# Early output tiles, the opening's loads in another order, and the opening joined with the first projection in one block

## The reference

```python
def first_block(x, c, ...):
    c_act = silu(c)
    for l in range(2):
        mod = c_act @ w_ada[l] + b_ada[l]
        shift, scale, gate = split(mod, 3)
        h = rms_norm(x, norm_g[l]) * (1.0 + scale) + shift
        proj = h @ w_in[l]
        gq, gk, gv, glr, gz, dq, dk, dv, dz = split_columns(proj)
        gq, gk, gv = split(silu(causal_depthwise_conv(concat(gq, gk, gv), conv_w[l])))
        o_gla = gla_branch(gq, gk, gv, glr, gz, ...)       # chunked gated linear attention
        lam = exp(sum(lam_q1 * lam_k1)) - exp(sum(lam_q2 * lam_k2)) + lam_init
        o_diff = diff_branch(dq, dk, dv, dz, ..., lam)     # softmax(map 0) - lam * softmax(map 1)
        x = x + gate * (concat(o_gla, o_diff) @ w_out[l])
    return x

def second_block(x, ...):        # MLA attention, short convolution and SSD side by side, then a gated FFN
    ...
```

## Time and profile before

| | before |
|---|---|
| median of 3 runs | 2401.17 us |
| profiled execution, its own time | 2397.69 us |
| its span | 2395.6 us |
| mean granted clock of PE | 0.997 |
| PE busy | 2314.5 us (97%) |
| DVE busy | 1263.4 us (53%) |
| ScalarE busy | 1064.2 us (44%) |
| GpSimd busy | 596.3 us (25%) |

### The profile page before, as it was taken

How to read it: one execution, slowest core, us unless ns; L and a number is a source line. 1 busy time by engine, 2 the same in 40 slices (tenths; PEclk the granted TensorE clock), 3 DMA queues, 4 the chain that set the end, 5 groups by cost and what they waited for, 6 DMA issues and landing times. The chain is left out here.

```text
span 2395.6 us, 33130 instructions
## 1 busy us (share of the span) xinstructions
PE 2314.5 (97%) x12824; PEld 1888.7 (79%) x12824; DVE 1263.4 (53%) x1776; ACT 1064.2 (44%) x2262; POOL 596.3 (25%) x411
## 2 busy tenths in 40 slices
PE   6999999989999999999999999999999999999999
PEld 4787787778887777777888887677888888888887
DVE  5855304874644411785551366660787777774121
ACT  4445333774534433575443445553653333334221
POOL 2200020232400021132332121212214444465130
PEclk9999999999999999999999999999999999999999
DMA  7442110104112111103211100003222222236231
GB/s 254 132 133 80 36 53 1 36 2 166 62 44 98 45 53 36 35 2 124 88 53 30 58 1 5 23 10 132 89 81 95 80 79 80 94 134 245 89 132 44
DMA packets 139073, 181.87 MB, mean 76 GB/s; under 512 B 8700, under 2 KB 102307, under 8 KB 138917
## 3 DMA queue, kind: packets, MB, share of 16 engines
q1 hardware_dynamic: 137877, 179.74, 22.2%
q10 hardware_dynamic: 1040, 0.00, 0.0%
HBM read 151.41 MB, written 28.31 MB: 75 GB/s over the span
## 5 line engine op out<-in xcount | busy, mean ns | idle before, releaser
L825 PE MATMUL ps<-w_hi,hT_hi 128*128 128x512 f32 (+1 forms) x384 | 142.2, 370 | 2.1 <-PEq L683 1.0
L825 PE MATMUL ps<-hT_hi,w_hi 128*128 128x512 f32 x360 | 141.2, 392 | 2.8 <-PEq L275 2.8
L825 PE MATMUL ps<-w_lo,hT_hi 128*128 128x512 f32 (+1 forms) x384 | 142.1, 370 | 0.0
L825 PE MATMUL ps<-w_hi,hT_lo 128*128 128x512 f32 (+1 forms) x384 | 142.0, 370 | 0.0
L825 PE MATMUL ps<-hT_lo,w_hi 128*128 128x512 f32 x360 | 140.6, 390 | 0.0
L4093 POOL TENSOR_TENSOR w_lo<-ffn_sums,w_hi 128x512 fp32r<-128x512 f32 x76 | 96.7, 1293 | 172.1 <-ACT w_hi L4275 172.1
L756 POOL TENSOR_TENSOR w_lo<-difp_raw,w_hi 128x2048 fp32r<-128x2048 f32 x8 | 36.8, 4603 | 386.6 <-ACT w_hi L725 386.6
L825 PE MATMUL ps<-hT_hi,w_lo 128*128 128x512 f32 x328 | 128.4, 391 | 0.0
L4143 PE MATMUL ps<-ffn_t_hi,w_hi 128*128 128x512 f32 x304 | 118.4, 389 | 0.7 <-DVE ffn_u L4452 0.7
L4143 PE MATMUL ps<-ffn_t_hi,w_lo 128*128 128x512 f32 x304 | 118.3, 389 | 0.0
L4143 PE MATMUL ps<-ffn_t_lo,w_hi 128*128 128x512 f32 x304 | 118.3, 389 | 0.0
(11 more groups left out here) (575 smaller groups left out, 6477.3 us busy)
## 6 DMA issues: line engine op xcount, KB each, us to landing
ffn_raw<-in_ffn_w_up SPq DMA_DIRECT2D x40, 512.0 KB, 4.8
mix_gla<-in_w_ada SPq DMA_DIRECT2D x32, 512.0 KB, 3.5
ffn_raw<-in_ffn_w_down SPq DMA_DIRECT2D x30, 512.0 KB, 4.6
xres<-big SPq DMA_DIRECT2D x24, 512.0 KB, 2.6
hid<-ffn_f SPq DMA_DIRECT2D x22, 512.0 KB, 2.6
ffn_sums<-hid SPq DMA_DIRECT2D x44, 256.0 KB, 3.9
glap_raw<-in_w_in SPq DMA_DIRECT2D x10, 1024.0 KB, 5.2
difp_raw<-in_w_in SPq DMA_DIRECT2D x10, 1024.0 KB, 5.0
```

The source lines that it names most:

```text
L825: mm = nc.tensor.matmul(out, l, r, start=(job.part != 1 and c == 0 and k == 0), stop=(job.evac and c == job.chunks - 1 and k == len(pairs) ...
```

## The change

Three things are changed.

*The attention's end.* `OUT_EARLY` becomes the list (4, 5, 0): PE does the GLA half of output tiles 4, 5 and 0 inside the attention stage. Tile 4 is cut into four pieces of three matmuls (one feature chunk each): one ahead of the turns of rounds 21, 22 and 23 of PE's loop, one behind the loop. Tile 5 stands behind `turn_y(6)`, tile 0 is cut in two halves around `turn_y(7)`. The tiles are split in the order (4, 0, 5, 1, 2, 3, 6, 7); ScalarE converts the first two (4 and 0) in rounds 15 and 16 of its loop, where GpSimd, not DVE, subtracts them.

*The opening's loads.* SP issues `w_ada` 4 and 5 before the lambda rows, then the second weight tile, `w_ada` 6 and 7, and the small rows of the second block last. ScalarE's `weight(1)` stands between the partial sums 4 and 5.

*One block.* The opening and the projection of layer 0 share a block. The new `OpenSeam` carries the waits of the projection: PE's first two units wait for feature chunks 6 and 7 of the first token half alone (14 of the 16 units), from unit 2 on for all 16, from unit 4 on for the second weight tile, the turned small rows and the gains; the other engines wait for everything. Job 0 of layer 0 goes by token halves (spread).

```diff
@@ -29,7 +29,7 @@
 RIGHT = "right"
-OUT_EARLY = 2
+OUT_EARLY = (4, 5, 0)
 PLAIN_EARLY = (4, 5, 0)
@@ -263,7 +263,38 @@
-def stage_open(nc, m, a, x, layer_rows, lam_rows, lam_src, jobs):
+class OpenSeam:
+
+
+    def __init__(self, s_hi, s_lov, s_lop, s_wlo, s_gain, s_later, groups):
+        self.s_hi, self.s_lov, self.s_lop, self.s_wlo, self.s_gain = s_hi, s_lov, s_lop, s_wlo, s_gain
+        self.s_later, self.groups = s_later, groups
+
+    def split(self, eng, units):
+        eng.wait_ge(self.s_hi, units)
+        eng.wait_ge(self.s_lov, units // 2)
+        eng.wait_ge(self.s_lop, units // 2)
+
+    def settled(self, eng):
+        self.split(eng, 2 * KC)
+        eng.wait_ge(self.s_wlo, 8)
+        eng.wait_ge(self.s_later, self.groups)
+
+    def staging_free(self, sp):
+        self.settled(sp)
+
+    def before(self, pe, g, half):
+        if g == 0:
+            self.split(pe, 2 * KC - 2)
+        if g == 2:
+            self.split(pe, 2 * KC)
+        if g == 4:
+            pe.wait_ge(self.s_wlo, 8)
+            pe.wait_ge(self.s_later, self.groups)
+            pe.wait_ge(self.s_gain, KC // 2)
+
+
+def stage_open(nc, m, a, x, layer_rows, lam_rows, lam_src, jobs, block):
@@ -312,7 +343,6 @@
         lam = Lambdas(nc, ctx, m, lam_rows, cols)
-        block = ctx.enter_context(nc.Block())
         PAIRS, UNITS, RING = KC // 2, 2 * KC, 2
@@ -356,15 +386,15 @@
             ada_tile(sp, 3)
-            cols.load_extra(sp)
             ada_tile(sp, 4)
             ada_tile(sp, 5)
+            cols.load_extra(sp)
+            sp.wait_ge(s_wlo, 4)
+            load_tile(sp, wraw, jobs[1], s_wraw)
+            ada_tile(sp, 6)
+            ada_tile(sp, 7)
             later.load_extra(sp)
             later.load(sp)
-            ada_tile(sp, 6)
-            ada_tile(sp, 7)
-            sp.wait_ge(s_wlo, 4)
-            load_tile(sp, wraw, jobs[1], s_wraw)
@@ -535,10 +565,10 @@
                     partial(u // 2)
+                    if u == 8:
+                        weight(1)
                     partial(u // 2 + 1)
                 shifted(u)
-                if u == 8:
-                    weight(1)
                 if u == 11:
@@ -626,6 +656,7 @@
             later.wait_extra(dve)
+        return OpenSeam(s_hi, s_lov, s_lop, s_wlo, s_gain, later.s_cols, len(groups))
@@ -1027,7 +1058,7 @@
         conv.pads(dve, q)
-        if opening:
+        if m.layer:
             dve.wait_ge(opening.w.s_lo, 4)
@@ -1047,7 +1078,7 @@
                   setup=lambda ctx, q: conv.setup(ctx, q, "glap"), dve_before=dve_before, dve_after=dve_after,
-                  sp_job=sp_job, begun=0 if opening else KC - 2, base=base, block=block, opening=opening, tail=scan)
+                  sp_job=sp_job, begun=0 if m.layer else KC - 2, base=base, block=block, opening=opening, tail=scan)
@@ -1939,6 +1970,8 @@
     TB, OB = 6, 7
+    SPLIT = (4, 0, 5, 1, 2, 3, 6, 7)
+    SPLIT_AT = {15: 0, 16: 1}
     with ExitStack() as ctx:
@@ -2021,9 +2054,19 @@
+            def other_half(i, chunks):
+
+                if chunks[0] == 0:
+                    pe.wait_ge(s_p, 2 * n_steps - (2 if i >= 4 else 0))
+                    held.wait_done(pe)
+                    pe.wait_ge(s_olo, SPLIT.index(i) + 1)
+                out_products(nc, m, ps[:, i, :], i, 0, (m.w_hi[:, 0, :], m.w_lo[:, 0, :]), chunks[0] == 0, False, chunks)
+
             for n in range(n_steps + 2):
...
                     scores(n + 1)
+                if n >= n_steps - 1:
+                    other_half(4, (n - n_steps + 1,))
                 for part in range(2):
@@ -2031,19 +2074,13 @@
                     turn_y(i, min(n, n_steps))
-            def other_half(i):
-
-                if i == 0:
-                    pe.wait_ge(s_p, 2 * n_steps)
-                    held.wait_done(pe)
-                pe.wait_ge(s_olo, i + 1)
-                out_products(nc, m, ps[:, i, :], i, 0, (m.w_hi[:, 0, :], m.w_lo[:, 0, :]), True, False)
-
             assert [i for i in range(NT) if st.last[i] + TURN_LAG >= n_steps + 2] == [NT - 2, NT - 1]
+            other_half(4, (3,))
             turn_y(NT - 2, n_steps)
-            other_half(0)
+            other_half(5, range(KC // 2))
+            other_half(0, (0, 1))
             turn_y(NT - 1, n_steps)
-            other_half(1)
+            other_half(0, (2, 3))
@@ -2079,13 +2116,13 @@
                         sums(i)
-            for i in range(NT):
-                if i == 2:
+            for k in range(len(SPLIT_AT), NT):
+                if k == len(SPLIT_AT) + 1:
                     for t in range(NT):
...
                             sums(t)
-                toks = slice(P * i, P * i + P)
-                dve.wait_ge(s_ohi, i + 1)
+                toks = slice(P * SPLIT[k], P * SPLIT[k] + P)
+                dve.wait_ge(s_ohi, k + 1)
                 nc.vector.tensor_tensor(m.hT_lo[:, 0:4, toks], other[:, :, toks], m.hT_hi[:, 0:4, toks].bitcast(F32),
@@ -2112,6 +2149,12 @@
                 held.low(pool, n)
+                if n in SPLIT_AT:
+                    k = SPLIT_AT[n]
+                    toks = slice(P * SPLIT[k], P * SPLIT[k] + P)
+                    pool.wait_ge(s_ohi, k + 1)
+                    pool.tensor_tensor(m.hT_lo[:, 0:4, toks], other[:, :, toks], m.hT_hi[:, 0:4, toks].bitcast(F32),
+                                       ALU.subtract).then_inc(s_olo, 1)
             for i in range(NT):
@@ -2137,6 +2180,11 @@
                 nc.scalar.activation(r[:, :], r[:, :], ACT.Exp, scale=-0.5).then_inc(s_rr, 1)
+
+            def split(order):
+                for k in order:
+                    toks = slice(P * SPLIT[k], P * SPLIT[k] + P)
+                    nc.scalar.activation(m.hT_hi[:, 0:4, toks], other[:, :, toks], ACT.Copy).then_inc(s_ohi, 1)
@@ -2155,15 +2203,13 @@
                 held.high(act, n)
+                if n in SPLIT_AT:
+                    split((SPLIT_AT[n],))
                 for i in ends(n, SUM_LAG):
                     norm(i)
-            def split(tiles):
-                for i in tiles:
-                    toks = slice(P * i, P * i + P)
-                    nc.scalar.activation(m.hT_hi[:, 0:4, toks], other[:, :, toks], ACT.Copy).then_inc(s_ohi, 1)
             act.wait_ge(s_s, n_steps)
-            split(range(4))
+            split(range(len(SPLIT_AT), 4))
             for i in range(NT):
@@ -2351,7 +2397,7 @@
-            w.first_columns(pe, mixed, range(OUT_EARLY))
+            w.first_columns(pe, mixed, OUT_EARLY)
             for i in range(NT):
@@ -4568,14 +4614,16 @@
-        glas = [gla_jobs(a["w_in"][l], l > 0) for l in range(DEPTH)]
+        glas = [gla_jobs(a["w_in"][l], True) for l in range(DEPTH)]
         diffs = [diff_jobs(a["w_in"][l]) for l in range(DEPTH)]
...
                    for l in range(DEPTH) for n in ("lam_q1", "lam_k1", "lam_q2", "lam_k2")]
-        stage_open(nc, m, a, m.big, [rows_of(l) for l in range(DEPTH)], lam_rows, lam_src, glas[0][:2])
-        block = opening = None
+        block = nc.Block()
+        block.__enter__()
+        opening = stage_open(nc, m, a, m.big, [rows_of(l) for l in range(DEPTH)], lam_rows, lam_src, glas[0][:2],
+                             block)
         for l in range(DEPTH):
@@ -4593,13 +4641,13 @@
-                if not block:
+                if not l:
                     retire(m)
...
                                   a["b_ada"][l, 2 * D:3 * D].rearrange("(c p) -> c p", c=1), base, block, opening,
-                                  None if block else scan)
-                if block:
-                    block.__exit__(None, None, None)
+                                  None if l else scan)
+                block.__exit__(None, None, None)
+                if l:
                     retire(m)
...
                         scan(c3, c3.enter_context(nc.Block()), None)
```

## The result

| | before | after |
|---|---|---|
| median, first comparison | 2401.18 us (2398.46 to 2406.40, 4 runs) | 2386.48 us (2385.65 to 2389.44, 4 runs) |
| ratio, 95% interval | | 0.9937 (0.9924 to 0.9949) |
| profiled execution | 2397.69 us, span 2395.6 | 2386.57 us, span 2384.8 |
| mean granted clock | 0.997 | 0.993 |
| PE busy | 2314.5 us | 2317.7 us |

The change makes the kernel 14.7 us faster by these medians. The prediction was 2385.0 us, with 2379.0 to 2392.5 as its range.

A forecast was written before the change was run, and what follows sets the result against it. PE, with work in 97% of the span, bounds the kernel. Gains 3.5 + 2.7 + 1.7 + 6.8 = 14.7 us off the profiled 2397.7 give 2383.0; plus 2.1, 2385.0 us, range 2379 to 2392.5.

The forecast's parts named there:

- plus 2.1: Whole run: timed runs lie 0.8 to 3.5 us above the profiled one; the middle, 2.1 us, was added.
- Part 1: Opening: earlier second weight load and ScalarE's instruction in idle time remove PE's wait at L436; gain 3.5 us.
- slack of 1.0 us: Opening: the weight conversion ends at 43.8, before partial sum 5 can start at 44.83, so it costs nothing.
- Rival A: Opening: the load gains nothing, landing at 46.4 with ScalarE idle 3.5 us instead; 2388.5 us, chance 0.12.
- D: Opening: second weight tile so late that ScalarE stops ahead of partial sum 5; slower, 2407 at 65 us; chance 0.03.
- Part 2: Seam of opening and first projection: PE goes on at 65.8 instead of 68.53; gain 2.7 us.
- DVE's lag: First projection: DVE starts later against PE, 3.9 us in all, covered by its 4.3 us of waits; cost 0, at most 1.
- Part 3: Behind the seam, 69 to 73 us: the slow clock stretch goes without both opening pauses; gain 1.7 us.
- Part 4: Attention's end: early output-tile matmuls fill PE's idle time; gain 3.4 us a layer, 6.8 in all.
- Rival B: Attention: the filling is given back through GpSimd hindering DVE or delayed steps, 3.4 to 5.0 us; 2389.2, chance 0.14.
- Rival C: Clock falls in one or two other places, or seam stays slow; 1.7 to 3.4 us more, 2387.5, chance 0.13.
- signs of being wrong: ScalarE waiting for the load until 46 us, PE waiting above 1.5 us for DVE's combine, clock under 0.7 somewhere new.

The follow-up runs named there:

- e12_weight_slack: Changed kernel with the second weight tile issued ahead of the lambda rows and converted by ScalarE behind partial sum 5; 2385.99 us, ratio 0.9931.
- e7_load_late: Changed kernel with the second weight tile loaded last again, ScalarE's weight instruction keeping its new place; 2395.93 us, ratio 0.9973.
- e1_loads: Kernel before with only the opening's new load order and ScalarE's second weight instruction between partial sums 4 and 5; 2396.01 us, ratio 0.9972.
- e2_join: Kernel before with only the opening and first projection in one block and job 0 by token halves; 2398.04 us, ratio 0.9984.
- e10_dve_low: Changed kernel with the two early subtractions on DVE, one round later, instead of GpSimd; 2388.92 us, ratio 0.9941.
- e6_weight_back: Changed kernel with ScalarE's second weight instruction back behind shifted tile 8, new load order kept; 2386.94 us, ratio 0.9938.
- e8_no_spread: Changed kernel with job 0 of layer 0 in the old order of units, token halves in turn; 2388.52 us, ratio 0.9946.
- e11_two_tiles: Changed kernel with output tiles 4 and 5 early, without tile 0; 2394.32 us, ratio 0.9963.
- e5_before_again: Kernel before, unchanged, run once more for a second trace; 2402.57 us in one execution.
- e3_attention: Kernel before with only the attention's end changed (three output tiles early, two early splits with GpSimd's subtraction); 2397.80 us, ratio 0.9977.

## Why the prediction was right

**The time.** 2385.0 was forecast, 2386.48 and 2386.70 measured. The forecast was 14.7 us less than the profiled execution, plus 2.1. The median fell by 14.7 in the first comparison; by the ratios it is 15.1 and 15.9 us. By the traces PE gained 16.0 us up to 1327: 0.7 at the start, 7.9 in parts 1 to 3 (forecast 7.9) and 7.4 behind them, where the two attentions are (forecast 6.8). That the time itself came within 1.5 us is in part luck. The sum alone gives 2383.0 for the trace, which took 2386.57, since it lost 5.2 us in the second block that the sum did not have; the 2.1 added for another reason, the start and the attentions made up for most of it.

**Part 1, the loads: right.** L436's wait is gone, 3.5 us. The load's use at 41.9 was forecast and is 42.54, although two steps were off. SP issued it at 33.90, not 32.2: the four issues of w_ada 2 to 5 in a row took until 27.53 (17.37 + 10.16), and the lambda rows, which had been issued ahead of w_ada 4 and 5, took 6.3 us behind them. And the load took 8.6 us, not 9.75. The slack of 1.0 us was in truth none: the conversion ended at 44.46 and partial sum 5 came right with its end. It cost PE 0.2 us, as e12_weight_slack shows. Rival A (chance 0.12) did not happen, and e7_load_late shows D's price.

**Part 2, one block: right.** The first matmul follows 0.38 us behind the start of the last turns. DVE's lag took 1.2 of its 4.3 us of idle time in the seventh and eighth tile, where I had put 3.9 on it, and PE did not notice.

**Part 3, the clock: right.** I laid the stretch on the pause of 2.8 us just ahead of it, but took its 1.7 us for both pauses gone, and e1_loads and e2_join show that both have to go. What failed was my later expectation for e2_join, which gave the join alone the 1.7 us. The size fits the first trace of before: from its first matmul to the end of its block the first projection took 206.9 us (61.47 to 268.33) instead of 208.4 (68.53 to 276.95), 1.6 less. The end of the block came 8.6 and 9.1 us earlier, where parts 1 to 3 make 7.9; the start, 0.7 and 1.0 us ahead, is the rest.

**Part 4, the attention: right.** 3.4 us a layer were forecast. PE's waits over layer 0's attention fell from 12.1 to 8.6 us, 3.5, and over layer 1's from 11.8 to 8.4. Rival B did not happen. GpSimd's work cost nothing that e10_dve_low could win back: DVE's two reductions beside its new subtraction took no longer than without it (2.34 and 2.35 us), and the subtraction took the 1.27 us of the others:

```profile
490.90 1.27 POOL L2156 TENSOR_TENSOR hT_lo<-mix_gla,hT_hi 128x512 fp32r<-128x512 f32 x1 [1.64 <-ACT hT_hi L2187]
```

**Rival C came true in the trace, not in the time.** The trace has two stretches in the second block that that of before has not, and lost 5.2 us by them; a clock under 0.7 in a new place (0.57 from 1490 us) was one of my signs of being wrong. In the times it cancels, since the kernel before has it too, in its second trace and, as far as the mean clocks tell, in nearly all executions. By the number alone C, with 2387.5, is nearer to 2386.48 than the forecast. That the base trace was a lucky one is what I could have seen in a fast clock of 0.997, but only beside other runs. The 2.1 us that I added for the distance of trace and median were too little: the first four runs lie 3.5 us above the trace in the median, the 27 of the later set 6.0.

The Trainium skill ("TensorE: Matmul & The Clock Gate", section "What's actually happening") has the same kernel ramp up at its start after different numbers of matmuls in different runs, since the window runs free. The runs agree for the places that come and go further on (the stretch near 365 us is in nine of fourteen traces), but not for the one near 1500 us: it stands in thirteen of fourteen, at the same step.

## What to carry to other kernels

A pause of PE is worth its length and, for the longer ones in this kernel, in most cases a slow stretch behind it (1.4 to 3 us more). Two pauses close together shared one stretch, so a trace in which one of them is removed may show less than half of what removing both gives. A wait read from one trace has a spread of its own: the one at L436 was 3.5 to 5.0 us in four. When work is taken out from behind the last step of a block, ask what it covered at the block's end. And before a trace is used as the base of a sum, compare its mean granted clock and time with a number of plain runs: here the first trace would have been the third fastest of 27.

## What the runs showed of the hardware

- The mixer stage of the second block ran 206.0 us without a slow stretch and 208.2 to 211.3 with one or two. No pause of over 1 us stands ahead of the one near 1500 us; what calls it up there, and why the first trace had none, stays open.
- Pauses of 0.6 us (e6_weight_back) and 1.09 us (e8_no_spread) had no slow stretch behind them, those of 1.96 (e11_two_tiles, in both layers) and 7.7 us had, and 2.8 (e1_loads) and 5.0 us (e2_join), each where it stood alone. Where both stood there was one stretch: behind the second in the first trace of before (3.5 and 2.8 us), behind the first in e5_before_again (3.9 and 2.8) and e3_attention (4.8 and 2.8). That the pauses call up the stretches is read from these cases; no run shows by what rule.
- The second weight tile's time from issue to use was 9.75 us behind w_ada 6 and 7 and 8.6 us ahead of them; issuing it 7.2 us earlier brought it 8.3 us sooner (50.82 to 42.54).
- Two reductions of DVE from PSUM took 2.34 us beside a subtraction of GpSimd (1.27 us) and 2.35 without one.
